# Gate tiles of the gated scan: who empties PSUM, and when the silu runs

## The chip, the cores and the metric

The kernel runs on one core of a Trainium2 chip. The core has five engines that run their own instruction streams and meet at semaphores: TensorE (PE, matrix products, results in PSUM), VectorE (DVE), ScalarE (ACT, functions from tables), GpSimd (POOL) and SyncE (SP, which issues the loads here). The time is that of one execution on the device in microseconds, the median of three runs.

## The reference

Two transformer-like blocks are applied to 1024 tokens of width 1024. The first block has two layers, and each mixes tokens by a gated linear scan beside a differential attention. The change lies in the stage of the gated scan, so it runs twice. What that stage computes:

```python
h = rms_norm(x, norm_g[l]) * (1.0 + scale[:, None]) + shift[:, None]
proj = h @ w_in[l]
gq, gk, gv, glr, gz, dq, dk, dv, dz = split_columns(proj)
...
log_a = jax.nn.log_sigmoid((glr @ w_gk + b_gk)) / GLA_GATE_TEMP     # per 64-token chunk:
b = jnp.cumsum(log_a, axis=2)
k_dec = k * jnp.exp(b_end[:, :, None] - b)
u = jnp.einsum('bnchk,bnchv->nbhkv', k_dec, v)
state = a_c[..., None] * state + u_c                                 # scan over chunks
o = jnp.einsum('bnchk,nbhkv->bnchv', q, states)
o = rms_norm(o, g_out).reshape(B, S, GLA_WIDTH)
return o * jax.nn.silu(z.astype(f32))
```

`z` here is `gz`, 1024 tokens by 512. The gate is `silu(z)`, and it is multiplied into the normed output.

## The kernel before

The stage is `stage_gla`. It treats the 1024 tokens as eight tiles of 128 and runs eleven steps n (`STEPS`), a software pipeline written out by hand: in step n the engines turn and gate tile n, decay and update the states for tile n-1, read out tile n-2 and turn back tile n-3. The code of each engine lists its instructions in that order, and semaphores hold them to one another.

Each step of TensorE also holds three units of another job, a plain projection, to fill it (`project`, line 1025). A unit is twelve matmuls of 128x512: one tile of 128 tokens against half of the 1024 features, each product split in three for precision. Four units (p0 to p3) run ahead of step 0, and step n holds p(4+3n) to p(6+3n). p0 to p15 make the gate z: p0 to p3 open tiles 0 to 3, p4 to p7 complete them (`s_unit`), p8 to p11 open tiles 4 to 7, p12 to p15 complete them. p16 to p31 make the values of the attention that follows, in the same way. All use four PSUM banks (`BANKS`), so p8 must wait until tile 0 has left bank 0, and so on. The semaphore for this is `s_zev`.

Before, ScalarE takes a gate tile out of PSUM with the silu on the way (`gates`, line 1196), into `zv` (in the trace `vd`): tiles 0 to 3 at the end of its step 1, tiles 4 to 7 at the end of its step 3. The silu needs another function table than the rest of the stage, so a table load stands ahead of the four and one behind them (L1197). The weights are split into a rounded part by ScalarE (`weights.high`, L920) and the rest by GpSimd.

What the prediction's steps touch, by name and line: on TensorE `turn` (transposes, L1043 and L1045), `gate` (L1052), `decays` (L1061, it waits for the next tile's keys and values, both copied out of the banks that it writes or that `turn` wrote), `states` (L1076), `outputs` (L1090), `turn_y` (L1101); on ScalarE `values` (L1150), `decays` (L1157), `squares` (L1174), `empty_y` (L1190); on VectorE `keys` (L1236), `decayed` (L1244), `log_gate` (L1251), `states` (L1265), `normed` (L1277, it reads the gate), `empty` (L1285, the value tiles), and at the end of each of its steps an accumulation for the modulation of the next layers, `mod.accumulate` (L824, four instructions of 128x256).

Of the kernel before, what the change touches and what calls it, by code (L numbers as in the profile page):

```python
# [19 lines left out]
ACT = mybir.ActivationFunctionType  # L20
# [75 lines left out]
def semaphores(nc, ctx, m, stage, names):  # L96

    out = [ctx.enter_context(nc.semaphore(f"{stage}{m.tag}_{n}")) for n in names.split()]
    m.used.extend(out)
    assert len(m.used) <= 157, len(m.used)  # L100
    return out
# [827 lines left out]
def stage_gla(nc, m, feat, glrT, zv, w_gk, b_gk, jobs, mod, slot):  # L929
# [8 lines left out]
    pairs = GLA_H // 2  # L938
    with ExitStack() as ctx:  # L939
        (s_w, s_turn, s_kv, s_gate, s_abs, s_act, s_la, s_suf, s_dec, s_kd, s_u, s_st, s_o, s_sq, s_r,  # L940
         s_y, s_yt, s_mix, s_dve, s_unit, s_slot, s_zev, s_vev, s_mraw0, s_mraw1, s_macc, s_spread, s_gated,
         s_own) = semaphores(
            nc, ctx, m, "gla", "w turn kv gate abs act la suf dec kd u st o sq r y yt mix dve unit slot zev vev mraw0 "
            "mraw1 macc spread gated own")

        def sb(name, shape):
            return ctx.enter_context(m.tensor("gla_" + name, shape, F32))
# [3 lines left out]
        la, dec = sb("la", [P, 2, GLA_QK]), sb("dec", [P, 2, GLA_QK])  # L951
# [4 lines left out]
        sq, ssq, r = sb("sq", [P, GLA_H, GLA_DV]), sb("ssq", [P, 2, GLA_H]), sb("r", [P, 2, GLA_H])  # L956
        y = sb("y", [P, 2, GLA_W])
        weights = ScanWeights(nc, ctx, m, "gla", jobs, [1 - slot, 1 - slot, slot, slot])
        ps = m.ps
# [5 lines left out]
        LEAD, UNITS, BANKS = 4, 4 * NT, 4  # L965
# [3 lines left out]
        def o_of(h):  # L969
            return ps[:, U[h % 2], P * (h // 2):P * (h // 2) + P]  # L970

        def unit(u):


            job, w = u // 16, u % 16
            block4 = w // 4
            second = block4 in (1, 2)
            tile = w % 4 + 4 * (block4 // 2)
            return job, tile, second, block4 % 2 == 0
# [4 lines left out]
        @block.sync  # L984
        def _(sp):
            sp.dma_start(wgk[0:RANK, :], w_gk).then_inc(s_w, 16)
            sp.dma_start(wgk[RANK:RANK + 1, :], b_gk).then_inc(s_w, 16)
            load_tile(sp, weights.raw, weights.jobs[0], weights.s_raw)
            for k in range(2):
                mod.load(sp, (s_mraw0, s_mraw1), s_macc, n0 + k, n0)  # L990
            for k in range(2, late):
                if k in (3, 5, 7):
                    w = (k - 1) // 2
                    sp.wait_ge(weights.s_lo, w)
                    load_tile(sp, weights.raw, weights.jobs[w], weights.s_raw)
                mod.load(sp, (s_mraw0, s_mraw1), s_macc, n0 + k, n0)
# [144 lines left out]
        @block.scalar  # L1141
        def _(act):
            act.preload_act_table_set(LN_EXP)
            own = Count(act, s_act)

            def values(i):
                act.wait_ge(s_turn, i + 1)
                if i >= 2:
                    act.wait_ge(s_u, i - 1)
                nc.scalar.activation(vtok[:, i % 2, :], ps[:, TB, :], ACT.Copy).then_inc(s_kv, 1)  # L1150

            def decays(i):
                act.wait_ge(s_suf, i + 1)
                if i >= 2:
                    act.wait_ge(s_kd, i - 1)
                    act.wait_ge(s_st, 4 * (i - 1))
                nc.scalar.activation(dec[:, i % 2, :], ps[:, TB, 0:GLA_QK], ACT.Exp).then_inc(s_dec, 1)  # L1157
                nc.scalar.activation(aend[:, i % 2, :], ps[:, TB, 256:260], ACT.Exp).then_inc(s_dec, 1)

            def gate(i):  # L1160

                act.wait_ge(s_gate, i + 1)
                if i >= 1:
                    act.wait_ge(s_la, i)
                own.mark(nc.scalar.activation(gexp[:, :], ps[:, KG, GLA_QK:2 * GLA_QK], ACT.Abs))
                own.settle()
                own.mark(nc.scalar.activation(gexp[:, :], gexp[:, :], ACT.Exp, scale=-1.0))
                own.settle()
                nc.scalar.activation(gexp[:, :], gexp[:, :], ACT.Ln, bias=1.0).then_inc(s_abs, 1)

            def squares(i):
                act.wait_ge(s_o, i + 1)
                for h in range(GLA_H):
                    own.mark(nc.scalar.activation(sq[:, h, :], o_of(h), ACT.Square, accum_out=ssq[:, i % 2, h:h + 1]))  # L1174

            def root(i):
                b = i % 2
                own.settle()

                if i >= 2:  # L1180
                    act.wait_ge(s_y, i - 1)
                own.mark(nc.scalar.activation(r[:, b, :], ssq[:, b, :], ACT.Ln, bias=m.eps[:, 0:1],
                                              scale=1.0 / (GLA_DK * GLA_DV)))
                own.settle()
                nc.scalar.activation(r[:, b, :], r[:, b, :], ACT.Exp, scale=-0.5,
                                     bias=m.ln_eighth[:, 0:1]).then_inc(s_r, 1)

            def empty_y(i):
                act.wait_ge(s_yt, i + 1)
                nc.scalar.activation(feat[:, 4:8, P * i:P * i + P], ps[:, TB, :].rearrange("p (h t) -> p h t", h=4),  # L1190
                                     ACT.Copy, scale=m.col(m.C_GLAG)).then_inc(s_mix, 1)

            def gates(tiles):
                for i in tiles:
                    act.wait_ge(s_unit, i + 1)
                    nc.scalar.activation(zv[:, i, :], ps[:, i % BANKS, :], ACT.Silu).then_inc(s_zev, 1)
                act.preload_act_table_set(LN_EXP)  # L1197

            weights.high(act, 0)
            for n in STEPS:  # L1200
                if 0 <= n - 2 < NT:
                    squares(n - 2)
                if n < NT:
                    values(n)
                if 0 <= n - 2 < NT:
                    root(n - 2)
                if 0 <= n - 1 < NT:
                    decays(n - 1)
                if n < NT:
                    gate(n)  # L1210
                if n >= 3:
                    empty_y(n - 3)
                if n == 1:
                    gates(range(4))
                if n == 2:
                    act.wait_ge(s_slot, 1)
                    weights.high(act, 1)
                if n == 3:
                    gates(range(4, 8))
                    weights.high(act, 2)  # L1220
                if n == 7:
                    act.wait_ge(s_slot, 2)
                    weights.high(act, 3)

        @block.vector
        def _(dve):
# [43 lines left out]
            def normed(i):  # L1270
                b = i % 2
                dve.wait_ge(s_r, i + 1)
                dve.wait_ge(s_zev, i + 1)
                if i >= 2:
                    dve.wait_ge(s_yt, i - 1)
                for h in range(GLA_H):
                    ins = nc.vector.scalar_tensor_tensor(out=y[:, b, P * h:P * h + P], in0=o_of(h),  # L1277
                                                         scalar=r[:, b, h:h + 1], in1=zv[:, i, P * h:P * h + P],
                                                         op0=ALU.mult, op1=ALU.mult)
                ins.then_inc(s_y, 1)  # L1280

            def empty(i):
                dve.wait_ge(s_unit, NT + i + 1)
                dve.wait_ge(s_y, i + 1)
                nc.vector.tensor_copy(zv[:, i, :], ps[:, i % BANKS, :]).then_inc(s_vev, 1)  # L1285
# [10 lines left out]
            for n in STEPS:  # L1296
                if n < NT:
                    keys(n)
                if 0 <= n - 2 < NT:
                    normed(n - 2)  # L1300
                if 0 <= n - 1 < NT:
                    decayed(n - 1)
                if n < NT:
                    log_gate(n)
                if 0 <= n - 1 < NT:
                    states(n - 1)
                sums(n)
                if n < late:
                    mod.accumulate(dve, (s_mraw0, s_mraw1), s_macc, n0 + n, n0)
                for u in range(LEAD + 3 * n, LEAD + 3 * n + 3):  # L1310
                    if 16 <= u < UNITS and not unit(u)[3]:
                        empty(unit(u)[1])

# [2594 lines left out]
```

## Time and profile before

| | us |
|---|---|
| runs | 2603.38, 2603.83, 2608.33 |
| median | 2603.83 |
| profiled execution | 2604.45 |
| its span | 2602.7 |
| TensorE busy | 2429.2 (93%) |
| VectorE busy | 1211.1 (47%) |
| ScalarE busy | 985.7 (38%) |
| GpSimd busy | 631.6 (24%) |

The span goes from the first to the last instruction. Busy time is what the engine's instructions cover. The scan of layer 0 lies at 170 to 311 us, that of layer 1 at 790 to 928 us. The granted clock is the share of TensorE's full 2.4 GHz, 0.5 being 1.2 GHz.

### The profile page before, as it was taken

What the parts mean: (1) busy time and instruction counts of PE and PEld (TensorE: products, weight loads), DVE (VectorE), ACT (ScalarE), POOL (GpSimd) and SP (SyncE); (2) the same over time, 40 slices, a digit from 0 to 9 for tenths busy, and PEclk for the clock granted to TensorE, in tenths of its full rate; (3) what the DMA queues carried; (4) which work ended last, traced back from release to release, by engine and by line L of the source; (5) the groups of instructions that cost most, each with busy time, mean ns of one, the idle gap of its engine ahead of it and who ended that gap; (6) DMA issues with size and microseconds to landing.
All of it is one profiled execution on the core that took longest, in us unless ns stands there. A gap on an engine that the chain in (4) does not pass through costs nothing. (4 is left out here: it accounts for less than half of the span.)

```text
span 2602.7 us, 32829 instructions
## 1 busy us (share of the span) xinstructions
PE 2429.2 (93%) x13084; PEld 1973.5 (76%) x13084; DVE 1211.1 (47%) x1660; ACT 985.7 (38%) x2097; POOL 631.6 (24%) x293
## 2 busy tenths in 40 slices
PE   4999999879998999887999999999999999999998
PEld 2876787668786777776878886667788888888886
DVE  5764403764652411584561366551653333333336
ACT  4224323663523432474433354553522121212123
POOL 3211120232311022032221130112333233333331
PEclk9999999899998999898999999999999999999999
DMA  6432010103112111002211100004111212121213
GB/s 217 132 116 77 28 62 1 33 7 140 65 41 66 66 49 33 17 18 98 89 57 27 54 1 9 17 10 154 65 45 37 65 33 65 33 65 33 65 39 147
DMA packets 130861, 154.54 MB, mean 59 GB/s; under 512 B 7308, under 2 KB 100883, under 8 KB 130709
## 3 DMA queue, kind: packets, MB, share of 16 engines
q1 hardware_dynamic: 127776, 152.05, 17.9%
q8 instruction: 104, 1.70, 0.3%
q10 hardware_dynamic: 2933, 0.39, 0.1%
q14 instruction: 48, 0.39, 0.1%
HBM read 135.65 MB, written 16.78 MB: 59 GB/s over the span
## 5 line engine op out<-in xcount | busy, mean ns | idle before, releaser
L695 PE MATMUL ps<-hT_hi,w_hi 128*128 128x512 f32 x1088 | 426.0, 392 | 16.2 <-DVE hT_lo L3419 5.8
L695 PE MATMUL ps<-hT_lo,w_hi 128*128 128x512 f32 x1088 | 424.8, 390 | 0.0
L695 PE MATMUL ps<-hT_hi,w_lo 128*128 128x512 f32 x1088 | 424.8, 390 | 0.0
L695 PEld LDWEIGHTS ps<-hT_hi,w_hi 128*128 128x128 f32 x1088 | 205.3, 189 | 60.3 <-issue 17.6
L695 PEld LDWEIGHTS ps<-hT_hi,w_lo 128*128 128x128 f32 x1088 | 205.1, 188 | 43.0
L695 PEld LDWEIGHTS ps<-hT_lo,w_hi 128*128 128x128 f32 x1088 | 205.2, 189 | 42.4
L631 POOL TENSOR_TENSOR w_lo<-ffn_raw,w_hi 128x2048 fp32r<-128x2048 f32 (+1 forms) x32 | 164.0, 5125 | 111.7 <-ACT w_hi L605 111.7
L3673 DVE TENSOR_SCALAR work<-work,fcols 128x1024 f32<-128x1024 f32 x44 | 33.2, 755 | 287.4 <-ACT work L3630 287.4
L3630 ACT ACTIVATE work<-ps 128x512 f32<-128x512 f32 x88 | 52.4, 597 | 279.7 <-PE ps L695 273.0
L605 ACT ACTIVATE w_hi<-ffn_raw 128x2048 fp32r<-128x2048 f32 (+1 forms) x32 | 59.6, 1864 | 247.1 <-PE ps L695 153.0
L3654 POOL TENSOR_TENSOR ffn_hid_lo<-work,ffn_hid_hi 128x1024 fp32r<-128x1024 f32 x22 | 64.9, 2949 | 346.8 <-ACT ffn_hid_hi L3644 346.8
L695 PE MATMUL ps<-w_hi,hT_hi 128*128 128x512 f32 (+1 forms) x384 | 142.9, 372 | 1.8 <-PEq L939 1.8
L695 PE MATMUL ps<-w_lo,hT_hi 128*128 128x512 f32 (+1 forms) x384 | 142.9, 372 | 0.0
L695 PE MATMUL ps<-w_hi,hT_lo 128*128 128x512 f32 (+1 forms) x384 | 142.6, 371 | 0.0
L1931 PE MATMUL ps<-w_hi,hT_hi 128*128 128x512 f32 x288 | 116.0, 403 | 11.6 <-DVE hT_lo L2125 8.6
L1025 PE MATMUL ps<-w_hi,hT_hi 128*128 128x512 f32 x256 | 111.4, 435 | 16.0 <-PEq L3729 9.4
L1931 PE MATMUL ps<-w_lo,hT_hi 128*128 128x512 f32 x288 | 115.0, 399 | 0.0
L1931 PE MATMUL ps<-w_hi,hT_lo 128*128 128x512 f32 x288 | 114.6, 398 | 0.0
L695 PE MATMUL ps<-w_lo,ffn_hid_hi 128*128 128x512 f32 x288 | 114.6, 398 | 0.0
L695 PE MATMUL ps<-w_hi,ffn_hid_hi 128*128 128x512 f32 x288 | 113.4, 394 | 0.0
L695 PE MATMUL ps<-w_hi,ffn_hid_lo 128*128 128x512 f32 x288 | 113.3, 393 | 0.0
L1025 PE MATMUL ps<-w_lo,hT_hi 128*128 128x512 f32 x256 | 104.7, 409 | 0.0
(496 smaller groups left out, 5331.4 us busy)
## 6 DMA issues: line engine op xcount, KB each, us to landing
ffn_raw<-in_ffn_w_up SPq DMA_DIRECT2D x40, 512.0 KB, 5.1
mix_gla<-in_w_ada SPq DMA_DIRECT2D x32, 512.0 KB, 3.7
xres<-big SPq DMA_DIRECT2D x24, 512.0 KB, 2.6
difp_raw<-in_w_in SPq DMA_DIRECT2D x10, 1024.0 KB, 5.0
ffn_raw<-in_ffn_w_down SPq DMA_DIRECT2D x10, 1024.0 KB, 5.1
open_ada<-in_w_ada SPq DMA_DIRECT2D x8, 1024.0 KB, 12.6
gla_wraw<-in_w_in SPq DMA_DIRECT2D x8, 1024.0 KB, 6.0
big<-xres SPq DMA_DIRECT2D x2, 4096.0 KB, 16.2
```

Of the source, the lines that this page charges most:

```text
L605: nc.scalar.activation(m.w_hi[:, (t + base) % 2, 0:w], raw[:, 0:w], ACT.Copy).then_inc(s_hi, 1)
L631: pool.tensor_tensor(m.w_lo[:, b, 0:w], raw[:, 0:w], m.w_hi[:, b, 0:w].bitcast(F32), ALU.subtract).then_inc(s_lo, 1)
L695: mm = nc.tensor.matmul(out, l, r, start=(job.part != 1 and c == 0 and k == 0), stop=(job.evac and c == job.chunks - 1 and k == 2))
L1025: mm = nc.tensor.matmul(out, l, r, start=(opens and c == 0 and k == 0), stop=(not opens and c == KC // 2 - 1 and k == 2))
L1931: mm = self.nc.tensor.matmul(out, l, r, start=(first and c == 0 and n == 0), stop=(last and c == KC // 2 - 1 and n == 2))
L3630: nc.scalar.activation(q.u[:, up, pad + 512 * half:pad + 512 * half + 512], psum, ACT.Copy).then_inc(q.free[g % NBANK], 1)
L3654: pool.tensor_tensor(ring[1][:, j % RING, :], q.f, ring[0][:, j % RING, :].bitcast(F32), ALU.subtract).then_inc(q.extra["hlo"], 1)
L3673: nc.vector.tensor_scalar(cv, src[:, 0:S], tap(j, 0, up), None, ALU.mult).then_inc(own, 1)
```

## The change

VectorE copies each of the eight gate tiles out of PSUM when it is complete (`empty_z`), at the end of its steps, as it did with the value tiles. ScalarE then runs one silu over four tiles that lie side by side in SBUF, in place. `s_zev` now counts VectorE's copies, and a new semaphore `s_silu` counts the two silu, for which `normed` waits.

```diff
-            def gates(tiles):
-                for i in tiles:
-                    act.wait_ge(s_unit, i + 1)
-                    nc.scalar.activation(zv[:, i, :], ps[:, i % BANKS, :], ACT.Silu).then_inc(s_zev, 1)
+            def gates(half):
+                tiles = zv[:, BANKS * half:BANKS * half + BANKS, :]
+                act.wait_ge(s_zev, BANKS * (half + 1))
+                nc.scalar.activation(tiles, tiles, ACT.Silu).then_inc(s_silu, 1)
                 act.preload_act_table_set(LN_EXP)
...
                 if n == 1:
-                    gates(range(4))
+                    gates(0)
                 if n == 2:
                     act.wait_ge(s_slot, 1)
                     weights.high(act, 1)
                 if n == 3:
-                    gates(range(4, 8))
+                    gates(1)
                     weights.high(act, 2)
...
                 dve.wait_ge(s_r, i + 1)
-                dve.wait_ge(s_zev, i + 1)
+                dve.wait_ge(s_silu, i // BANKS + 1)
...
-            def empty(i):
+            def empty_z(i):
+                dve.wait_ge(s_unit, i + 1)
+                nc.vector.tensor_copy(zv[:, i, :], ps[:, i % BANKS, :]).then_inc(s_zev, 1)
+
+            def empty_v(i):
                 dve.wait_ge(s_unit, NT + i + 1)
                 dve.wait_ge(s_y, i + 1)
                 nc.vector.tensor_copy(zv[:, i, :], ps[:, i % BANKS, :]).then_inc(s_vev, 1)
...
                 for u in range(LEAD + 3 * n, LEAD + 3 * n + 3):
-                    if 16 <= u < UNITS and not unit(u)[3]:
-                        empty(unit(u)[1])
+                    if u < UNITS and not unit(u)[3]:
+                        (empty_v if unit(u)[0] else empty_z)(unit(u)[1])
```

VectorE's queue in layer 0, from the accumulation of step 0 to the keys of step 2, before. The names in brackets are the semaphores that an instruction waits for:

```order
134 L824 SCALAR_TENSOR_TENSOR gate<-mix_gla,cact,gate 128x256 [waits gla0_mraw0]
135 L824 SCALAR_TENSOR_TENSOR gate<-mix_gla,cact,gate 128x256 [waits gla0_macc] x3
136 L1236 COPY gla_ktok<-ps 128x256 [waits gla0_turn]
137 L1244 TENSOR_TENSOR gla_kdec<-gla_ktok,gla_dec 128x256 [waits gla0_kv,gla0_dec]
138 L1251 SCALAR_TENSOR_TENSOR gla_la<-ps,gla_gexp 128x256 [waits gla0_abs]
139 L1265 SCALAR_TENSOR_TENSOR gla_state<-gla_state,gla_aend,ps 128x128 [waits gla0_u,gla0_dec]
140 L1265 SCALAR_TENSOR_TENSOR gla_state<-gla_state,gla_aend,ps 128x128
141 L1265 SCALAR_TENSOR_TENSOR gla_state<-gla_state,gla_aend,ps 128x128 [waits gla0_st]
142 L1265 SCALAR_TENSOR_TENSOR gla_state<-gla_state,gla_aend,ps 128x128
143 L824 SCALAR_TENSOR_TENSOR gate<-mix_gla,cact,gate 128x256 [waits gla0_macc,gla0_mraw1]
144 L824 SCALAR_TENSOR_TENSOR gate<-mix_gla,cact,gate 128x256 [waits gla0_macc] x3
145 L1236 COPY gla_ktok<-ps 128x256 [waits gla0_kd,gla0_turn]
```

The same stretch of VectorE's queue after the change, from the last accumulation of step 0:

```order
135 L824 SCALAR_TENSOR_TENSOR gate<-mix_gla,cact,gate 128x256 [waits gla0_macc] x3
136 L1284 COPY vd<-ps 128x512 [waits gla0_unit] x3
137 L1236 COPY gla_ktok<-ps 128x256 [waits gla0_turn]
138 L1244 TENSOR_TENSOR gla_kdec<-gla_ktok,gla_dec 128x256 [waits gla0_kv,gla0_dec]
139 L1251 SCALAR_TENSOR_TENSOR gla_la<-ps,gla_gexp 128x256 [waits gla0_abs]
140 L1265 SCALAR_TENSOR_TENSOR gla_state<-gla_state,gla_aend,ps 128x128 [waits gla0_u,gla0_dec]
141 L1265 SCALAR_TENSOR_TENSOR gla_state<-gla_state,gla_aend,ps 128x128
142 L1265 SCALAR_TENSOR_TENSOR gla_state<-gla_state,gla_aend,ps 128x128 [waits gla0_st]
143 L1265 SCALAR_TENSOR_TENSOR gla_state<-gla_state,gla_aend,ps 128x128
144 L824 SCALAR_TENSOR_TENSOR gate<-mix_gla,cact,gate 128x256 [waits gla0_macc,gla0_mraw1]
145 L824 SCALAR_TENSOR_TENSOR gate<-mix_gla,cact,gate 128x256 [waits gla0_macc] x3
146 L1284 COPY vd<-ps 128x512 [waits gla0_unit]
```

Three copies stand ahead of the keys of step 1, and the fourth, tile 3, behind the accumulation of step 1. In the same way one copy (tile 4) ends step 2 and three (tiles 5 to 7) end step 3.

ScalarE's queue in layer 0, from the last part of gate(1) to values(2), before:

```order
102 L1169 ACTIVATE gla_gexp<-gla_gexp 128x256 [waits gla0_act]
103 L1196 ACT_TABLE_LOAD
104 L1196 ACTIVATE vd<-ps 128x512 [waits gla0_unit] x4
105 L1197 ACT_TABLE_LOAD
106 L1174 ACTIVATE gla_sq,gla_ssq<-ps 128x128 [waits gla0_o]
107 L1174 ACTIVATE gla_sq,gla_ssq<-ps 128x128 x3
108 L1150 ACTIVATE gla_vtok<-ps 128x512 [waits gla0_u,gla0_turn]
```

The same rows of ScalarE after the change:

```order
102 L1169 ACTIVATE gla_gexp<-gla_gexp 128x256 [waits gla0_act]
103 L1196 ACT_TABLE_LOAD
104 L1196 ACTIVATE vd<-vd 128x2048 [waits gla0_zev]
105 L1197 ACT_TABLE_LOAD
106 L1174 ACTIVATE gla_sq,gla_ssq<-ps 128x128 [waits gla0_o]
107 L1174 ACTIVATE gla_sq,gla_ssq<-ps 128x128 x3
108 L1150 ACTIVATE gla_vtok<-ps 128x512 [waits gla0_u,gla0_turn]
```

The four instructions became one that waits for VectorE; what stands ahead of it and behind it is the same. In step 3 it is the same again, with `weights.high` behind the second table load.

## Rows read from the trace of the kernel before

**Rows 1.** The page, busy time of TensorE (share of span, instructions).

```profile
PE 2429.2 (93%) x13084; PEld 1973.5 (76%) x13084; DVE 1211.1 (47%) x1660; ACT 985.7 (38%) x2097; POOL 631.6 (24%) x293
```

**Rows 2.** Waits of TensorE, 165 to 320 us: total, times, longest.

```profile
PE ps L1025 <- ACT vd L1196: 3.3, 1, 3.3
PE ps L1061 <- ACT gla_vtok L1150: 2.1, 1, 2.1
PE ps L1061 <- DVE gla_ktok L1236: 0.9, 1, 0.9
```

**Rows 3.** Timeline of TensorE, steps 1 and 2: start, length, instruction [idle before].

```profile
197.64 0.69 PE L1052 MATMUL ps<-gla_wgk,glrT 17*128 17x256 f32 x2
201.61 0.50 PE L1025 MATMUL ps<-w_hi,hT_hi 128*128 128x512 f32 x1 [3.28 <-ACT vd L1196]
...
206.15 0.68 PE L1076 MATMUL ps<-gla_vtok,gla_kdec 64*64 64x128 f32 x16
...
209.71 0.68 PE L1090 MATMUL ps<-gla_state,big 64*64 64x128 f32 x16
...
213.79 0.59 PE L1061 MATMUL ps<-gla_la,suffix 128*128 128x256 f32 x2
...
214.66 0.69 PE L1052 MATMUL ps<-gla_wgk,glrT 17*128 17x256 f32 x2
215.28 0.50 PE L1025 MATMUL ps<-w_hi,hT_hi 128*128 128x512 f32 x1
...
218.22 0.68 PE L1076 MATMUL ps<-gla_vtok,gla_kdec 64*64 64x128 f32 x16
```

**Rows 4.** Timeline of VectorE, both layers, and the line of the value copies.

```profile
194.22 0.42 DVE L1236 COPY gla_ktok<-ps 128x256 f32<-128x256 f32 x1 [2.63 <-PE ps L1045]
...
208.15 2.04 DVE L824 SCALAR_TENSOR_TENSOR gate<-mix_gla,cact,gate 128x256 f32<-128x256 f32 x4
...
226.39 0.42 DVE L1236 COPY gla_ktok<-ps 128x256 f32<-128x256 f32 x1
...
233.52 2.04 DVE L824 SCALAR_TENSOR_TENSOR gate<-mix_gla,cact,gate 128x256 f32<-128x256 f32 x4
...
885.36 1.28 DVE L1285 COPY vd<-ps 128x512 f32<-128x512 f32 x2
...
L1285 DVE COPY vd<-ps x16: 678/680/692, 264.3 to 927.8; 128x512 f32<-128x512 f32 x16
```

**Rows 5.** Timeline of ScalarE, steps 3 and 4 of layer 0.

```profile
234.77 2.07 ACT L1196 ACTIVATE vd<-ps 128x512 f32<-128x512 f32 x4
236.85 1.28 ACT L1197 ACT_TABLE_LOAD   x1
238.15 1.91 ACT L920 ACTIVATE w_hi<-gla_wraw 128x2048 fp32r<-128x2048 f32 x1
239.97 0.26 ACT L1174 ACTIVATE gla_sq<-ps 128x128 f32<-128x128 f32 x1
```

**Rows 6.** Timeline of TensorE, steps 3 and 4 of layer 0.

```profile
226.95 0.67 PE L1061 MATMUL ps<-gla_la,suffix 128*128 128x256 f32 x2 [0.93 <-DVE gla_ktok L1236]
...
241.72 0.67 PE L1061 MATMUL ps<-gla_la,suffix 128*128 128x256 f32 x2 [2.08 <-ACT gla_vtok L1150]
...
243.29 0.79 PE L1025 MATMUL ps<-w_hi,hT_hi 128*128 128x512 f32 x1
...
247.80 0.68 PE L1076 MATMUL ps<-gla_vtok,gla_kdec 64*64 64x128 f32 x16
```

**Rows 7.** Busy time by stretch: us, engines, granted clock, DMA share, GB/s.

```profile
202.00:206.00 4.00, 4.00 (x12) 2.96 (x10) 0.00 (x0) 2.31 (x4) 0.00 (x0) 0.57 0.00 0
242.00:246.00 4.00, 4.00 (x14) 3.04 (x13) 3.15 (x6) 1.76 (x6) 2.67 (x1) 0.66 0.00 0
```

**Rows 8.** Timeline of TensorE, step 1 of layer 1.

```profile
821.90 0.80 PE L1025 MATMUL ps<-w_hi,hT_hi 128*128 128x512 f32 x1 [3.28 <-ACT vd L1196]
...
827.16 0.68 PE L1076 MATMUL ps<-gla_vtok,gla_kdec 64*64 64x128 f32 x16
```

More of the change, by code:

```diff
@@ L940, in stage_gla @@
         (s_w, s_turn, s_kv, s_gate, s_abs, s_act, s_la, s_suf, s_dec, s_kd, s_u, s_st, s_o, s_sq, s_r,
-         s_y, s_yt, s_mix, s_dve, s_unit, s_slot, s_zev, s_vev, s_mraw0, s_mraw1, s_macc, s_spread, s_gated,
+         s_y, s_yt, s_mix, s_dve, s_unit, s_slot, s_zev, s_silu, s_vev, s_mraw0, s_mraw1, s_macc, s_spread, s_gated,
          s_own) = semaphores(
-            nc, ctx, m, "gla", "w turn kv gate abs act la suf dec kd u st o sq r y yt mix dve unit slot zev vev mraw0 "
+            nc, ctx, m, "gla", "w turn kv gate abs act la suf dec kd u st o sq r y yt mix dve unit slot zev silu vev mraw0 "
             "mraw1 macc spread gated own")
```

## The prediction

> **What bounds the kernel now.** I read the page first, then TensorE's waits in the stretch of the gated scan, then the timelines of TensorE, VectorE and ScalarE there, and last the granted clock in short stretches. TensorE is busy 93% of the span [rows 1], so time is won or lost where TensorE stands, or where its clock is low. The scan runs twice, once a layer. Within 165 to 320 us, the first of them, TensorE waits in three places for another engine: 3.3 us for ScalarE's silu of a gate tile, 2.1 us for ScalarE's copy of the values, 0.9 us for VectorE's copy of the keys [rows 2]. The second layer shows the same three. I number the scan's steps n as the code does and call its projection units p0, p1, ...
>
> The first wait is the one that the change touches: gate(1), the second step's gate matmul, starts at 197.64 and p8 at 201.61 after 3.28 us idle, because bank 0 must be empty and ScalarE empties it only behind that step's decays, gate and a table load [rows 3]. It costs more than its length. p8 to the state matmuls behind it takes 4.54 us (201.61 to 206.15), where a like unit takes 2.94 (215.28 to 218.22) [rows 3]: the granted clock is 0.57 in 202 to 206, mostly the 1.2 GHz level [rows 7]. So it costs 3.28 + 1.60 = 4.88 us in layer 0. In layer 1 the same stretch is 5.26 us (821.90 to 827.16) [rows 8], so 3.28 + 2.32 = 5.60. Removing it alone would give 10.5 us.
>
> **The change, part by part.**
>
> *The wait at p8 goes.* VectorE copies tiles 0 to 2 at the end of step 0, and p8, p9 and p10 need just those. The third copy waits for p6, the last unit ahead of the transposes on which VectorE's next instruction, keys(1), waits; VectorE idles 2.63 us before keys(1) at 194.22, and gate(1), which needs the keys, comes only at 197.64 [rows 3, 4]. Those 3.4 us hide a copy of 0.68, so I price these three at nothing. Without that cover gate(1) would start later by what keys(1) is late, at most 0.68.
>
> *The same wait comes back two matmul groups later.* ScalarE now waits for four copies before one silu. The fourth copy (tile 3) stands on VectorE behind the state updates and the accumulation of step 1. Behind the waiting silu stand on ScalarE the reload of the Ln/Exp table, the four squares of step 2 and values(2), and TensorE's decays(1) waits for values(2). Walk it in layer 0. TensorE: gate(1) 197.64, p8 0.62 later (214.66 to 215.28) at 198.26, state matmuls +2.94 at 201.20, outputs(0) +3.56 (206.15 to 209.71) at 204.76, ready for decays(1) +4.08 (209.71 to 213.79) at 208.84 [rows 3]. VectorE: accumulation 2.00 behind the state matmuls (206.15 to 208.15), 203.20; it lasts 2.04, and neighbours overlap by 0.08, so the copy starts at 205.16; the copy is 0.68, ends 205.84 [rows 3, 4]. ScalarE: start about 0.1 later (an estimate from TensorE, which starts 0.14 after the keys' copy ends, 226.39 + 0.42 to 226.95), silu 128x2048, then the table load 1.30 start to start (236.85 to 238.15), then 1.75 from the first square to decays(3) (239.97 to 241.72) [rows 5, 6].
> The merged silu from SBUF is not in the trace. The nearest row of its size is ScalarE's 128x2048 copy from SBUF, 1.91 us; four silu of 128x512 from PSUM take 2.07 [rows 5]. These are the ends; I take 1.92, near the lower, since size and source are the same. So 205.94 + 1.92 + 1.30 + 1.75 = 210.91: a new wait of 2.07 us, and decays(1) starts 2.88 us earlier than its 213.79. In layer 1 the walk is the same from gate(1), which leaves 0.72 more: 3.60 earlier.
>
> *The clock behind that new wait.* The trace has a wait of this size before the same instruction: 2.08 us before decays(3) at 241.72. The unit behind it takes 4.51 us (243.29 to 247.80) instead of 2.94, with a granted clock of 0.66 in 242 to 246 [rows 6, 7]. So I price the new wait at 1.57 more per layer; the other end is nothing.
> The Trainium skill (TensorE: Matmul & The Clock Gate, Why this matters for your kernels) ties the return to the low clock to idle stretches longer than this one. By it this term would be zero and the sum +0.8 us. The trace does not agree with it: the 2.08 us wait was followed by such a long unit in both layers.
>
> *One copy more in step 2.* Tile 4 is complete in step 2, so VectorE's copy stands between that step's accumulation and keys(3). keys(3) starts right behind the accumulation (226.39) and decays(2) already waits 0.93 for it, starting at 226.95 [rows 4, 6]. One copy in a row of copies is 0.64 (two in 1.28 [rows 4]): +0.64 per layer, and the wait becomes 1.57. Lower end zero if something else ends it; no gain is possible, since the copy stands in line. Whether the clock falls after 1.57 us no row says: 0.93 did not do it, 2.08 did. Ends 0 and 1.57; I take 0, and keep the other for a rival.
>
> *Step 3 gets later.* Before, ScalarE runs its four silu at 234.77, without a wait. After the change it waits for tiles 5, 6 and 7, which VectorE copies behind the accumulation of step 3: 233.52 + 1.96 + 3 x 0.64 + 0.04 = 237.44, ScalarE 237.54, 2.77 later; the shorter silu (1.92 for 2.08 to the next start) gives back 0.16. The fourth silu of before reads p15's tile and starts three quarters into the 2.07 us, about 236.3; so p15 is complete before the last copy would start (236.76), and the copies bound it. Behind the silu stand the table load, the weights' rounding (238.15), the squares and values(4), and decays(3) waits for these already: 2.08 becomes 4.69. +2.61 per layer [rows 4 to 6].
> The unit behind it took 4.51. Behind the longer waits it took 4.54 and 5.26 [rows 3, 8]. I add 0.4 of a possible 0.75.
>
> Nothing hangs on the rest. The weight residuals of GpSimd and the loads behind them move with ScalarE and are needed steps later; the value copies of the second job stand where they stood. ScalarE is busy less (0.16 four times), which nobody waits for.
>
> **Sum.** Layer 0: -2.88 + 1.57 + 0.64 + 2.61 + 0.40 = +2.34. Layer 1: -3.60 + 1.57 + 0.64 + 2.61 + 0.40 = +1.62. Together +4.0 us. The profiled execution took 2604.45 (span 2602.70, 1.75 around it), so it becomes 2608.4; the median of the runs is 2603.83, 0.6 below it, so I forecast 2607.8.
>
> **Rivals.**
>
> *The clock stays up behind the 2.07 us wait.* For it: the stretch before is busier than before decays(3), since a wait is gone. Against it: two waits of 2.08 both dropped it. 3.96 - 3.14 = +0.8, 2604.6. Chance 0.20. It is also what that page of the Trainium skill would make of it.
>
> *Slower: the clock falls a third time.* The place is p14 in step 3, behind the 1.57 us wait for keys(3). From some wait between 0.93 and 2.08 us the clock falls for the unit behind it, and it decides there: +1.57 per layer, and with the full 0.75 behind the long wait another 0.7 in all. 4.0 + 3.1 + 0.7 = +7.8, 2611.6. Against it: 1.57 is only halfway. Chance 0.23. To this I count that ScalarE's silu table load runs behind the wait, not ahead of it. In the instruction order the load carries no wait, so I give that 0.04 of the 0.23; it would cost 1.28 at two places per layer, 4.0 + 5.1 = +9.1, 2612.9.
>
> *Faster: the wait goes and does not come back.* If decays(1) and decays(3) are not bound by ScalarE, because VectorE gets to its copies sooner than I walked, there remain -4.88 - 5.60 + 2 x 0.64 = -9.2, 2594.6. For it: 93% busy TensorE and a real wait removed. Against it: the copies stand in line behind an accumulation that depends on TensorE's state matmuls. Chance 0.07.
>
> *The change doesn't do what it says.* p8 could still wait, now for a copy by VectorE. Against it: tile 0 is complete one step earlier. Chance too small to carry a number; it would be my sum without the gains, +10 and more, and stands within the slower case.
>
> **How the numbers follow.** My forecast has 0.50. A difference under 0.2%, 5.2 us, is about what a measurement of this kernel can't tell from no change. The forecast (+4.0, its own spread 2 to 6) lies mostly within: 0.44 of its 0.50, and 0.06 above. The clock that stays up (0.20) is wholly within, the third fall (0.23) above, the faster case (0.07) below. So faster 0.07, same 0.64, slower 0.29. The range from 2601.0 to 2612.5 holds both neighbours and leaves out the faster case and the late table load.
>
> **What would show it.** In the changed profile: no wait before p8, and p8 to p10 at full clock. A wait of about 2 us for the values before decays(1), followed by a unit of 4.5 us. A wait of 1.6 for the keys before decays(2). 4.7 us before decays(3) in place of 2.1. ScalarE's silu 1.9 us long, started right after a copy on VectorE, with its table load long done. The prediction is wrong if decays(1) follows p10 without a wait, if the wait before decays(3) stays near 2, or if the unit behind decays(1) takes 2.9 us.

## The result and the profile after

| | before | changed |
|---|---|---|
| median of 6 runs, us | 2604.64 | 2612.82 |
| lowest to highest, us | 2603.07 to 2608.33 | 2609.16 to 2618.27 |
| ratio, 95% interval | | 1.0033, 1.0023 to 1.0044 |
| profiled execution (span), us | 2604.45 (2602.7) | 2609.16 (2607.4) |

The changed kernel is slower by 0.33%, some 8.6 us (6.0 to 11.5 by the interval), where I had forecast 4.0 and no change clear of noise. The direction of the sum was right, its size half of what came.

The waits came almost as walked. These are TensorE's waits in the scan of layer 0, 165 to 320 us of the changed kernel (total, times, longest); they answer to [rows 2]:

```profile
PE ps L1061 <- ACT gla_vtok L1150: 6.4, 2, 4.5
PE ps L1025 <- PEq L3733: 5.0, 1, 5.0
PE ps L1061 <- DVE gla_ktok L1236: 1.5, 1, 1.5
```

The wait at p8 is gone, and the wait for the values is there twice. The 5.0 us of L1025 stand at the start of the stage, as before. Now TensorE's timeline there (start, length, instruction, idle before), which answers to [rows 3, 6]:

```profile
198.65 0.69 PE L1052 MATMUL ps<-gla_wgk,glrT 17*128 17x256 f32 x2
199.27 0.50 PE L1025 MATMUL ps<-w_hi,hT_hi 128*128 128x512 f32 x1
...
202.21 0.68 PE L1076 MATMUL ps<-gla_vtok,gla_kdec 64*64 64x128 f32 x16
...
205.77 0.68 PE L1090 MATMUL ps<-gla_state,big 64*64 64x128 f32 x16
...
211.90 0.67 PE L1061 MATMUL ps<-gla_la,suffix 128*128 128x256 f32 x2 [1.88 <-ACT gla_vtok L1150]
...
217.99 0.68 PE L1076 MATMUL ps<-gla_vtok,gla_kdec 64*64 64x128 f32 x16
...
227.32 0.67 PE L1061 MATMUL ps<-gla_la,suffix 128*128 128x256 f32 x2 [1.52 <-DVE gla_ktok L1236]
...
231.83 0.68 PE L1076 MATMUL ps<-gla_vtok,gla_kdec 64*64 64x128 f32 x16
...
244.56 1.19 PE L1061 MATMUL ps<-gla_la,suffix 128*128 128x256 f32 x2 [4.55 <-ACT gla_vtok L1150]
...
246.33 1.22 PE L1052 MATMUL ps<-gla_wgk,glrT 17*128 17x256 f32 x2
247.48 0.79 PE L1025 MATMUL ps<-w_hi,hT_hi 128*128 128x512 f32 x1
...
252.17 0.68 PE L1076 MATMUL ps<-gla_vtok,gla_kdec 64*64 64x128 f32 x16
```

Two things are to be seen. p8 follows gate(1) at once, and it runs at full rate (199.27 to 202.21, 2.94 us). And the stretch from `decays` to `states`, 4.51 us at full clock (227.32 to 231.83), takes 6.09 behind the wait of 1.88 (211.90 to 217.99) and 7.61 behind the wait of 4.55 (244.56 to 252.17). In layer 1 it is 7.63 behind both:

```profile
834.18 0.67 PE L1061 MATMUL ps<-gla_la,suffix 128*128 128x256 f32 x2 [1.88 <-ACT gla_vtok L1150]
...
841.81 0.68 PE L1076 MATMUL ps<-gla_vtok,gla_kdec 64*64 64x128 f32 x16
...
851.14 0.67 PE L1061 MATMUL ps<-gla_la,suffix 128*128 128x256 f32 x2 [1.52 <-DVE gla_ktok L1236]
...
868.38 0.67 PE L1061 MATMUL ps<-gla_la,suffix 128*128 128x256 f32 x2 [4.55 <-ACT gla_vtok L1150]
...
869.50 1.21 PE L1052 MATMUL ps<-gla_wgk,glrT 17*128 17x256 f32 x2
870.64 0.79 PE L1025 MATMUL ps<-w_hi,hT_hi 128*128 128x512 f32 x1
...
876.01 0.68 PE L1076 MATMUL ps<-gla_vtok,gla_kdec 64*64 64x128 f32 x16
```

The granted clock in these stretches of the changed kernel (columns as in [rows 7], the clock is the third number from the end):

```profile
212.00:218.00 6.00, 6.00 (x21) 4.38 (x22) 1.91 (x6) 1.94 (x6) 0.00 (x0) 0.72 0.01 1
228.00:232.00 4.00, 4.00 (x22) 2.88 (x26) 1.06 (x3) 1.67 (x5) 0.00 (x0) 1.00 1.01 373
244.00:252.00 8.00, 7.43 (x20) 5.57 (x20) 2.46 (x6) 2.57 (x8) 3.48 (x1) 0.57 0.00 0
834.00:842.00 8.00, 7.82 (x27) 5.52 (x31) 1.98 (x6) 2.27 (x9) 0.00 (x0) 0.57 0.00 0
```

Behind the long wait the engine is at its 1.2 GHz level nearly all the way. In layer 0 even the first small matmuls, those of `decays`, take 1.19 us for what took 0.67 [rows 6]; in layer 1 they still take 0.67, and the gate's behind them 1.21 for 0.69. Behind the wait of 1.88 it is so for about half of the stretch in layer 0 and for nearly all of it in layer 1.

ScalarE and VectorE in layer 0 of the changed kernel show the cause that I had named (answer to [rows 4, 5]):

```profile
200.68 1.28 ACT L1196 ACT_TABLE_LOAD   x1
206.90 1.92 ACT L1196 ACTIVATE vd<-vd 128x2048 f32<-128x2048 f32 x1 [4.93 <-DVE vd L1284]
...
233.85 1.28 ACT L1196 ACT_TABLE_LOAD   x1
237.77 1.92 ACT L1196 ACTIVATE vd<-vd 128x2048 f32<-128x2048 f32 x1 [2.64 <-DVE vd L1284]
```

```profile
206.18 0.68 DVE L1284 COPY vd<-ps 128x512 f32<-128x512 f32 x1
...
235.85 1.88 DVE L1284 COPY vd<-ps 128x512 f32<-128x512 f32 x3
```

The table is loaded ahead of the wait, ScalarE then stands 4.93 and 2.64 us for VectorE's last copy, and the merged silu takes 1.92 us.

### The profile page after: what moved, and what is told of

It is laid out like the page before. It is cut to its first block and busy times, and to the rows that moved or that the text cites. A ratio compares the mean times of both kernels' runs of the same rounds, so it can differ in the third digit from the quotient of the medians.

```text
span 2607.4 us, 32835 instructions
## 1 busy us (share of the span) xinstructions
PE 2430.9 (93%) x13084; PEld 1973.0 (76%) x13084; DVE 1220.4 (47%) x1676; ACT 985.1 (38%) x2085; POOL 632.2 (24%) x293
## 5 line engine op out<-in xcount | busy, mean ns | idle before, releaser
L1025 PE MATMUL ps<-w_hi,hT_hi 128*128 128x512 f32 x256 | 111.0, 434 | 9.4 <-PEq L3733 9.4
L1025 PE MATMUL ps<-w_lo,hT_hi 128*128 128x512 f32 x256 | 104.6, 409 | 0.0
```

Of the source, the lines that this page charges most:

```text
L1025: mm = nc.tensor.matmul(out, l, r, start=(opens and c == 0 and k == 0), stop=(not opens and c == KC // 2 - 1 and k == 2))
```

## The experiments

There are ten runs, the first of them the changed kernel once more. Each kernel was timed 5 to 11 times beside the kernel before; the times are medians. Ratios are to the kernel before, with 95% intervals; where kernels of different runs are compared, the ratios count.

**e1_again**, the changed kernel once more, no edit.

> The changed kernel once more, as a control. Theory A (the size that was off is the clock behind the two new waits of TensorE): the waits in the scan are the same to 0.1 us (1.9, 1.5 and 4.6 us in each layer), while the time that the unit behind each takes differs from the first profile, between 2.9 and 5.4 us; time near 2612.8. Theory B (the excess comes from elsewhere in the kernel): both the waits and the units behind them repeat to 0.1 us and the total moves all the same.

Measured: 2613.85, ratio 1.0039 (1.0025 to 1.0052). The waits repeat: 1.88, 1.50 and 4.54 in layer 0, 1.88, 1.52 and 4.52 in layer 1. What follows them doesn't. In layer 1 of this execution:

```profile
833.19 0.67 PE L1061 MATMUL ps<-gla_la,suffix 128*128 128x256 f32 x2 [1.88 <-ACT gla_vtok L1150]
...
837.70 0.68 PE L1076 MATMUL ps<-gla_vtok,gla_kdec 64*64 64x128 f32 x16
...
847.02 0.67 PE L1061 MATMUL ps<-gla_la,suffix 128*128 128x256 f32 x2 [1.52 <-DVE gla_ktok L1236]
...
853.12 0.68 PE L1076 MATMUL ps<-gla_vtok,gla_kdec 64*64 64x128 f32 x16
```

The same 1.88 us that cost 3.12 more in the first profile cost nothing here (4.51), and the 1.52 us that had cost nothing cost 1.59 (6.10). So the waits repeat and the units behind them don't, as theory A has it; theory B, by which both repeat, falls. One profile shows one draw of the clock term.

**e2_three**, the first silu over the three tiles already copied, the second over five.

```diff
                 if n == 1:
-                    gates(0)
+                    gates(0, 3)
                 if n == 3:
-                    gates(1)
+                    gates(3, 8)
```

> The first silu covers tiles 0 to 2, which VectorE has copied a step earlier, the second tiles 3 to 7. Theory A: the wait of 1.88 us before decays(1) goes, and with it the low clock behind it (1.6 us in layer 0, 3.1 in layer 1); the wait before decays(3) grows by 0.43 for the fifth tile, to 5.0 us. 2 x 1.88 + 4.7 - 2 x 0.43 = 7.6 us under the changed kernel, about 2605. Theory C (VectorE's eight copies are the cost, not where the silu stands): within 1 us of the changed kernel, about 2613.

Measured: 2604.45, ratio 0.9998 (0.9989 to 1.0006), expected 2605. The wait before decays(1) is gone, that before decays(3) is 4.97 in both layers. VectorE's copies are all still there, so theory C falls: that the first silu no longer waits for tile 3, which is copied late in step 1, is worth all of the change's loss.

**e3_late**, the second silu in step 4.

```diff
+                if n == 4:
+                    gates(1)
                 if n >= 3:
                     empty_y(n - 3)
...
                 if n == 3:
-                    gates(1)
+                    act.wait_ge(s_unit, NT)
                     weights.high(act, 2)
```

> The second silu stands in step 4 between ScalarE's gate(4) and empty_y(1), where ScalarE is idle 4.4 us in the trace; the rounding of the next weights stays in step 3 and waits for p15. Theory A: the wait of 4.55 us before decays(3) and the low clock behind it (3.1 us) go in both layers, 15.3 us under the changed kernel, about 2597.5. Theory C: about 2613. In between, near 2603, if the table loads and the silu only move the wait to decays(4).

Measured: 2596.82, ratio 0.9972 (0.9961 to 0.9983), expected 2597.5. TensorE no longer waits before decays(3) or decays(4); the waits of 1.88 and of 1.5 to 1.6 us stay.

**e4_both**, the edits of e2 and e3 together.

> Both edits: silu of tiles 0 to 2 in step 1, of tiles 3 to 7 in step 4. Theory A: the two waits and their clock go, 7.6 + 0.9 + 15.3 = 23.8 us under the changed kernel, about 2589, and 15 us under the kernel before. TensorE's only wait left in the scan is the 1.5 us for keys(3). Theory C: about 2613. If the two waits share one cost (the clock recovers only once), clearly less than the sum of the two edits.

Measured: 2587.12, ratio 0.9933 (0.9921 to 0.9945), expected 2589. The gains add. ScalarE in step 4 of layer 0:

```profile
238.71 0.42 ACT L1169 ACTIVATE gla_gexp<-gla_gexp 128x256 f32<-128x256 f32 x1
239.15 1.28 ACT L1196 ACT_TABLE_LOAD   x1
240.44 2.34 ACT L1196 ACTIVATE vd<-vd 128x2560 f32<-128x2560 f32 x1
242.80 1.28 ACT L1197 ACT_TABLE_LOAD   x1
244.09 0.69 ACT L1190 ACTIVATE big<-ps,cols 128x512 f32<-128x512 f32 x1
```

Both table loads and five tiles of silu, 4.9 us, fill the gap between gate(4) and `empty_y`, and no wait of TensorE answers to them.

**e5_fill_after**, spare matmuls in the changed kernel's two waits for ScalarE.

```diff
+            def fill(count, bank, free):
+                if free:
+                    pe.wait_ge(s_zev, free)
+                for _ in range(count):
+                    nc.tensor.matmul(ps[:, bank, :], m.hT_hi[:, 0, 0:P], m.hT_hi[:, 0, 0:512], start=True, stop=True)
...
+                if n == 2:
+                    fill(8, 3, 4)
+                if n == 4:
+                    fill(19, 1, 6)
```

> The changed kernel, with TensorE given spare matmuls where it waits for ScalarE: 8 of 128x512 before decays(1), 19 before decays(3), into PSUM banks that are free and are overwritten later. The waits stay as long, only TensorE is busy in them. Theory A (a good part of the loss is the clock behind the waits): the stretches decays(1) to states and decays(3) to states take 4.5 us in both layers, in place of 4.5 to 7.6; 2 x (1.8 + 3.1) = 9.8 us under the changed kernel, about 2603.5. Theory D (the waits alone are the loss, the clock falls as often for other reasons): within 2 us of 2613.

Measured: 2604.39, ratio 1.0007 (0.9998 to 1.0016), expected 2603.5. TensorE in layer 0, where the spare matmuls stand ahead of the first and the last `decays` shown:

```profile
209.31 0.67 PE L1061 MATMUL ps<-gla_la,suffix 128*128 128x256 f32 x2
...
213.86 0.68 PE L1076 MATMUL ps<-gla_vtok,gla_kdec 64*64 64x128 f32 x16
...
223.19 0.67 PE L1061 MATMUL ps<-gla_la,suffix 128*128 128x256 f32 x2 [1.52 <-DVE gla_ktok L1246]
...
229.27 0.68 PE L1076 MATMUL ps<-gla_vtok,gla_kdec 64*64 64x128 f32 x16
...
242.01 0.67 PE L1061 MATMUL ps<-gla_la,suffix 128*128 128x256 f32 x2 [0.21 <-ACT gla_vtok L1160]
...
246.56 0.68 PE L1076 MATMUL ps<-gla_vtok,gla_kdec 64*64 64x128 f32 x16
```

decays(1) starts no earlier against gate(1) (209.31 - 196.06 = 13.25, as in the changed kernel, 211.90 - 198.65), so nothing was gained in the wait itself. Behind both filled waits the stretch is 4.55, in layer 1 it is 4.51. So work that serves nobody gives back 7 to 8 us by the ratios (1.0033 and 1.0039 against 1.0007): that much of the changed kernel's time is the clock behind these two waits. The unfilled wait for the keys now costs 1.57 behind it (6.08), and 2.86 in layer 1, where the stretch is 7.37.

**e6_fill_before**, the same in the kernel before: `fill(14, 4, 0)` before p8 in step 1, `fill(9, 1, 6)` before decays(3).

> The kernel before with the same spare matmuls in its own two waits: 14 before p8 and 9 before decays(3). Theory A: the clock loss of 1.6 to 2.3 behind p8 and 1.6 behind decays(3) goes in both layers, 7.1 us under the kernel before, about 2597. With the clock out of both kernels, e5 should stand above this one by the waits alone: 2 x (1.88 + 1.52 + 4.55) - 2 x (3.28 + 0.93 + 2.08) = +3.3 us. Theory D: about 2604, and e5 above it by the full 9.

Measured: 2597.49, ratio 0.9976 (0.9967 to 0.9985), expected 2597: 6.3 us of the kernel before were clock. But e5 stands 6.9 above it, not 3.3. The clock behind the wait for keys(3), which only e5 still lost (1.57 + 2.86 = 4.4 us in its profile; none in e6), would make 7.7. e10 tests that.

**e7_no_silu**, the changed kernel without the silu and its table loads; the gate enters the product as it is, so the kernel leaves out a part of the computation. As in e3, the next weights' rounding waits for the last gate unit instead.

> The changed kernel without the silu and its table loads (the gate is multiplied in as it is), VectorE's eight copies all kept; the next weights' rounding waits for p15. Theory A: as e4, since there the silu and its loads stand in idle time: within 2 us of 2587. Theory C (ScalarE's work is not hidden even in e4): 2 to 6 us below e4.

Measured: 2587.4, ratio 0.9941 (0.9929 to 0.9954), beside e4's 0.9933 (0.9921 to 0.9945). The silu and its loads cost nothing measurable where e4 has them. VectorE's eight copies per layer are in both, and both are 15 to 17 us below the kernel before.

**e8_acc**, e4 with VectorE's accumulations moved.

```diff
-                if n < late:
-                    mod.accumulate(dve, (s_mraw0, s_mraw1), s_macc, n0 + n, n0)
+                for k in {2: (), 3: (2,), 4: (3, 4)}.get(n, (n,)):
+                    if k < late:
+                        mod.accumulate(dve, (s_mraw0, s_mraw1), s_macc, n0 + k, n0)
```

> e4, and VectorE's accumulation of step 2 moved to step 3, that of step 3 to step 4, so that keys(3) follows tile 4's copy at once. Theory A: the wait of 1.5 us for keys(3) goes in both layers: 3.0 us under e4, about 2584, perhaps 1 more for the clock that sometimes falls behind it. Rival: VectorE's two accumulations in step 4 hold keys(5) and the wait comes back there: same as e4.

Measured: 2603.79, ratio 1.0002 (0.9993 to 1.0011), 17 us above e4 and far from both expectations. The wait for keys(3) is gone, and this is in its place, TensorE and then ScalarE and SyncE's queue in layer 0:

```profile
239.78 1.19 PE L1061 MATMUL ps<-gla_la,suffix 128*128 128x256 f32 x2 [6.17 <-ACT gla_vtok L1150]
```

```profile
236.21 1.91 ACT L920 ACTIVATE w_hi<-gla_wraw 128x2048 fp32r<-128x2048 f32 x1 [8.79 <-DMA gla_wraw<-in_w_in]
```

```profile
205.35 24.57 SPq L810 DMA_DIRECT2D mix_gla<-in_w_ada  x2
229.96 0.51 SPq L553 DMA_DIRECT2D gla_wraw<-in_w_in  x1
```

The raw weights for ScalarE's next rounding stand in SyncE's queue behind a load of modulation weights that waits until accumulation 2 has freed its buffer. Moving VectorE's accumulation moved that load to 229.96; in e4 it was issued at 223.06. The two waits (6.17 and 5.90 us) and the clock behind them (3.25 and 2.95), less the two waits of 1.5 that are gone, make 15 of the 17 us. I had not followed the moved step into SyncE's queue.

**e9_acc_sp**, e8 with the load of these raw weights one place earlier.

```diff
-                if k in (3, 5, 7):
-                    w = (k - 1) // 2
+                if k in (3, 4, 7):
+                    w = {3: 1, 4: 2, 7: 3}[k]
```

> e8 with the raw weights of the third job loaded ahead of the fifth part of the modulation weights, so that SyncE's queue no longer holds them back until VectorE's moved accumulation. Theory A: the 6 us wait of e8 for ScalarE, which sat 8.8 us on that load, goes, and the 1.5 us wait for keys(3) stays away: 3.0 us and up to 2 us of clock under e4, about 2583. Rival: the weights land later than p15 ends, and a wait of 1 to 2 us is left before decays(3): as e4, 2587.

Measured: 2585.12, ratio 0.9917 (0.9904 to 0.9931), against e4's 0.9933 (0.9921 to 0.9945): 4 us by the ratios, 2 by the medians, and the intervals overlap, so that e9 is faster than e4 is likely and not shown. TensorE waits for no other engine in either scan. It has the lowest ratio of all versions, 0.8% under the kernel before.

**e10_fill_acc**, the changed kernel with e5's spare matmuls and the accumulations and load order of e9.

> The changed kernel with the spare matmuls of e5 and the accumulations and the load order of e9, so that its wait for keys(3), behind which the clock still fell in e5, is gone. Only the two waits for ScalarE are left, both filled. Theory A (waits and the clock behind them are all there is): 2 x (1.88 + 4.55) = 12.9 us of waits, against 12.6 in e6, so within 1.5 us of e6, about 2597.8. Theory B (something of the change lies outside the waits): over 2 us above e6.

Measured: 2599.1, ratio 0.9976 (0.9966 to 0.9985), the same ratio as e6. With the clock out of both kernels and the wait for the keys gone, nothing of the change shows that the waits don't account for (12.9 against 12.6 us). Theory B, a cost outside the waits, is not borne out; the two intervals would still hide some 3 us.

## Why the prediction was wrong

Measured from gate(1) to outputs(3), the scan of the first profile is longer by 3.36 us in layer 0 (256.13 - 198.65 against 251.76 - 197.64) and by 4.12 in layer 1. My terms, in their order:

| term, us per layer | forecast | layer 0 | layer 1 |
|---|---|---|---|
| decays(1) starts earlier | -2.88 / -3.60 | -2.90 | -3.63 |
| clock behind the new wait | +1.57 | +1.58 | +3.12 |
| tile 4's copy ahead of keys(3) | +0.64 | +0.59 | +0.59 |
| silu late in step 3 | +2.61 | +2.47 | +2.47 |
| clock behind the longer wait | +0.40 | +1.53 | +1.53 |
| sum | +2.34 / +1.62 | +3.3 | +4.1 |

**Right, and shown:** the wait at p8 goes with its clock loss; the fourth copy stands late on VectorE, the silu behind it holds values(2) (wait 1.88, walked 2.07), and e2 removes that; one copy delays keys(3); three copies delay the second silu (wait 4.55, walked 4.69), and e3 removes that; the table load stands ahead of the wait, against the part of a rival that I gave 0.04. The three first copies are hidden: gate(1) follows decays(0) by 0.87 us as before. The waits sum to 15.9 us against 12.6 in the kernel before, +3.3, where the walk had 4.1.

**The step that failed** is the price of the clock behind the longer wait before decays(3), in the prediction's words "I add 0.4 of a possible 0.75". It came to 1.53 in both layers. I took the possible extra from the 3.28 us wait, whose next unit was 4.54 and 5.26, and looked only at the projection unit. In layer 0 that unit took 4.69 (247.48 to 252.17), hardly more than the 4.51 before; the other 1.35 us lie ahead of it, in `decays` and the gate's matmuls, which now ran at the low clock too. In layer 1 they split as 0.69 ahead of the unit and 0.84 in it.

For the other new wait, "I price the new wait at 1.57 more per layer": behind 1.88 us the three profiles of kernels that have it (the first, e1, e3) show 1.6, 3.1, 1.6, 0, 1.6 and about 3 us, 1.8 in the mean. My 1.57 was a fair mean and a poor bound, and that layer 0 hit it to 0.01 is luck.

The rival of a third fall, behind the wait for keys(3), had a place that is real and a threshold that is not. That wait of 1.5 to 1.6 us stands unfilled in seven profiles, twice in each. Of the 14 instances four paid: one of two in e1 (1.6 us) and in e3 (3.0), both in e5 (1.6 and 2.9), none in the first profile, e2, e4 and e7. That is a risk per wait, 0.6 us in the mean, and I had made it a yes or no and taken the no into the forecast.

With these means the sum would have been: waits +3.3; clock behind the waits of the changed kernel 2 x (1.8 + 0.6 + 3.1) = 11.1 us against 7.1 before, +4.0; together +7.3, within the measured interval. The forecast fell short by 4.6. The low price of the long wait is 2.3 of it (2 x 1.13), the other two prices 0.5 and 1.3, the waits came 0.8 shorter than walked, and 1.3 us are left, which is inside the interval.

**The two parts of the change.** The spare matmuls take out the clock behind the waits that they fill. The kernel before loses 6.3 us to it (e6). The changed kernel stands 0.57% to 0.63% above e10, 15 to 16 us, of which 3.0 are the waits for the keys that e10 lacks: 12 to 13 us of clock. So the change is +3.3 from waits and about +6 from the clock. That this adds up to the measured 9 to 10 us (ratios 1.0033 and 1.0039) is no test, because the same ratios went into it; the test is that e10 and e6 come out alike. My forecast had +4.1 from waits and, summed over both kernels, nothing from the clock: 7.1 us before and 7.1 after. The profiles show 7.1 before and, in the changed kernel, 10.9 (the first) and 9.3 (e1), where both profiled executions were the fastest of their run.

The profiled execution shows less than the median: its span grew by 4.7 us while its two scans grew by 7.5, so it was 2.8 shorter elsewhere. It is also the lowest of the six. Its granted clock over the span was 0.967, that of the other five 0.962 to 0.965. Where the other executions lose time, in the scans or outside, was not traced and stays open.

**The range** ended at 2612.5, 0.3 below the measured median. The third-fall case, 2611.6, was its upper pillar, and that case still held the long wait's price at 0.75. With 1.53 there it would have been 2613.2.

## What to carry to other kernels

A batch in front of a late input moves everything queued behind it on that engine: before merging four instructions into one that waits for the last of them, look at what stands behind it, and put the merged one where the engine is idle. Here VectorE's copies with a merged silu were worth +0.3% in one place of ScalarE's queue and in one grouping, and -0.7% in another (e4). Price a wait of TensorE as its length plus what the clock takes from all matmuls behind it, and treat the second part as a draw with a spread; spare matmuls in the wait show how large it is. A moved step also moves the loads that its buffers release.

## What the runs showed of the hardware

The same wait at the same place is not always followed by the same clock. The 1.88 us before decays(1), in three kernels whose code of the stage is the same up to there, were followed by 0, 1.6 or about 3.1 us of loss, in 5 of 6 instances by some. The 1.5 to 1.6 us before decays(2) were followed by 0, 1.6 or about 3, in 4 of 14 by some. The 2.08 us before decays(3) in the kernel before were followed by 1.6 both times. Waits of 4.5 to 5.0 us were followed by 3.0 to 3.8 us in all six instances, the two of 5.90 and 6.17 us in e8 by 2.95 and 3.25. At 0.93 us no loss was seen in the kernel before or in e6. What decides between the values was not found. The Trainium skill (TensorE: Matmul & The Clock Gate, Why this matters for your kernels) warns of longer gaps than 1.5 to 2 us; by the instances above the traces do not agree that such waits are safe.

GpSimd's weight residual (L925) and VectorE's accumulation of step 2 get in each other's way, before and after the change: the four instructions of L824 take 6.26 us where the residual runs beside them, and 2.04 elsewhere. Where e8 to e10 moved the accumulation away, it took 2.04 and the residual 4.6 instead of 4.8. This is what holds keys(3) in every version but e8 to e10. From the changed kernel:

```profile
219.99 6.26 DVE L824 SCALAR_TENSOR_TENSOR gate<-mix_gla,cact,gate 128x256 f32<-128x256 f32 x4
...
220.10 4.82 POOL L925 TENSOR_TENSOR w_lo<-gla_wraw,w_hi 128x2048 fp32r<-128x2048 f32 x1 [36.02 <-ACT w_hi L920]
```

The silu in SBUF took 1.49 us over 1536 elements per partition (e2, e4), 1.92 over 2048 (the changed kernel) and 2.34 over 2560 (e2, e4), so a tile more costs 0.43. A table load took 1.28 us each time.
